# The streams' tile first, the prompt's output projection in the gather rounds: a one-layer encoder step

## The chip, the cores and the metric

The kernel runs on one core of a Trainium2 chip. The metric is device time in microseconds (us). Three executions of the kernel before took 1362.1 us in the median (1358.86 to 1366.68).

## The reference, cut to what matters

384 tokens pass one layer: 256 of a prompt (tiles 0 and 1, of 128 tokens) and 16 each of 8 running streams (tile 2). All is float32.

```
xn = rmsnorm(x);  q,k,v,o,gates, aq,ak,av, iq,ik,iw = split(xn @ w_in)
h_m = mlstm(q, k, v, gates, state) * sigmoid(o)      # 4 heads; new C, n, m are outputs
idx = top_k(indexer scores of iq, ik, iw)            # 64 keys (prompt), 36 (streams)
h_a = softmax(aq . ak[idx] + bias) . av[idx]         # 8 heads, streams with their caches
h   = x + concat(h_m, h_a) @ w_out                   # output projection
hn  = rmsnorm(h)
s   = (hn @ w_pq) . subkeys                          # 8 heads x 2 halves x 128 subkeys
top 16 of each half -> 256 pairs -> top 16 per head  # 128 experts per token, gates by softmax
y   = rmsnorm(h + sum_k gate_k * gelu(pu[e_k] . hn) * pv[e_k])
```

`pu` and `pv` are stored side by side as `peer_uv`, 8 KB per expert. One gather fetches, for each of a tile's 128 tokens, the row of one expert: 1 MB. There are 3 tiles x 128 = 384 gathers, 402.68 MB.

## The kernel before, in words

Everything lives in one arena of on-chip memory with offsets written by hand. The order of the work on each engine is written out; the list `psum_plan` names each use of the six rotating accumulator banks in TensorE's order and which engine reads it (a bank is refilled when the one six names back was read). The last two banks sum up a tile's experts.

*Front.* TensorE turns x, then projects `small` (indexer keys, gates), mq, mk, mv, mo; from then on `head_steps` interleaves the four mLSTM heads (G, ST, NUM, CN) with the projections aq, ak, av, iq. A 128x384 projection group is 8 multiplications (L854), a 128x512 one for mv, mo, av likewise (L860). The indexer, the logits and the softmax of streams and prompt follow, with the output projection's first half `ya` (heads of mLSTM, four multiplications of the eight, L974) of all three tiles between them, then the second half `y`. VectorE computes in that stretch the selections (`keep_top`), the softmaxes, the additions into xr (`add_mix`) and the norms (`norm_h`). `output_gates` (L1320) turns mo of all three tiles in one reciprocal.

*Queries and routing.* `stream_queries` (L1094, `qs`, four chunks of w_pq for tile 2), `scores` (L1103, `sc`) and `prompt_query` (L1112, `qq`, 16 groups for tiles 0 and 1). VectorE's `route_subkeys`, `route_pairs` and `route_experts` turn scores into expert numbers; `route_experts(part)` signals `idx_ok`, at which GpSimd (L621) begins to gather. A part of `PARTS` is (tile, first head, heads): always four heads. ACT takes the exponential of the gates in `gate_exp`, in its order.

*Gather rounds.* Tile 2 goes first (`ORDER = (2, 0, 1)`). Its 16 rounds use 8 slots of 1 MB. For each slot: the gather lands, VectorE's `dots` (L1562), ScalarE's gelu, weight and diagonal (L774, L776, L782), TensorE's `weigh` (L1123: two 128x512 multiplications), then `used` lets GpSimd (L586, L587) gather into that slot again. Ahead of round i TensorE does `query_steps()[i]`, behind the dots of round i VectorE does `routing_steps()[i]`. Tiles 0 and 1 then run in 8 rounds of 16 slots each (GpSimd L604, L610, L611). `finish` adds the sum, norms the tile and releases its output.

A float32 multiplication is two instructions in the profile, so "x8" below is four of them, and a slot's two are "x4".

Of the kernel before, what the change touches and what calls it, by code (L numbers as in the profile page):

```python
# [12 lines left out]
U32 = mybir.dt.uint32  # L13
# [4 lines left out]
P = 128  # L18
# [30 lines left out]
LATE = 5  # L49
# [4 lines left out]

def head_steps():

    return [("G", 0), ("aq", 0), ("G", 1), ("ST", 0), ("aq", 1), ("NUM", 0), ("aq", 2), ("CN", 0), ("aq", 3),
# [3 lines left out]

def psum_plan():
    plan = []

    def add(eng, *names):
        plan.extend((n, eng) for n in names)

    for t in range(NT):
        add("V", f"xT{t}0", f"xT{t}1")
    add("V", "bvec")
    add("A", "small", "mq0")
    add("V", "iw")
    add("A", *[f"mq{g}" for g in range(1, 4)], *[f"mk{g}" for g in range(4)])
    add("V", *[f"mv{t}" for t in range(NT)])
    add("A", *[f"mo{t}" for t in range(NT)])
    add("V", "cols")
    add("A", "winter")  # L80
    add("V", "decay", "mkt0", "mkt1", "mkt2")
    for what, k in head_steps():
        add("A" if what == "ak" else "V", *([f"CN{k}{i}" for i in range(3)] if what == "CN" else [f"{what}{k}"]))
    add("A", "hmT0", "hmT1", "hmT2")

    add("V", "wht", "ri0", "ri1", "ri2", "isc")
    add("A", *[f"rp0{j}" for j in range(JP)])
    add("A", *[f"rp1{j}" for j in range(JP)])

    first, *others = ORDER  # L90
    ya = [f"ya{t}{i}" for t in ORDER for i in range(2)]
    add("V", *ya[:3], "lg0", "lg1", "lg2", *[f"lp0{j}" for j in range(JP)])
    add("V", *ya[3:5])
    add("A", "pTp0", "pTp1", "pTn0", "pTn1", "pp00", "pp01")

    add("V", *[f"lp1{j}" for j in range(JP)], ya[5], "oS0", "oS1", "op00", "op01", f"y{first}0", f"y{first}1")
    add("A", "pp10", "pp11", "pp12", "pp13")
    add("V", "op10", "op11")

    add("A", f"hnT{first}0", f"hnT{first}1", "qs0")  # L100
    add("V", f"y{others[0]}0", f"sc{first}0")
    add("A", "qs1")
    add("V", f"y{others[0]}1", f"sc{first}1", f"y{others[1]}0", f"y{others[1]}1")
    add("A", "qs2")
    for t in others:
        add("A", f"hnT{t}0", f"hnT{t}1")
    for what, *k in sum(query_steps(), []):
        add("V" if what == "sc" else "A", what + "".join(map(str, k)))
# [12 lines left out]

def routing_steps():

    steps = [None, ("subkeys", ORDER[0], 2), ("subkeys", ORDER[0], 3), ("pairs", ORDER[0], 4), ("experts", 1, 4, 4)]
    for n, t in enumerate(ORDER[1:]):
        steps += [("subkeys", t, 0), ("subkeys", t, 1), ("pairs", t, 0), ("experts", 2 + 2 * n, 0, 4),
                  ("subkeys", t, 2), ("subkeys", t, 3), ("pairs", t, 4), ("experts", 3 + 2 * n, 4, 4)]
    assert len(steps) == ROUNDS + LATE
    return steps  # L130

PARTS = [(t, h0, 4) for t in ORDER for h0 in (0, 4)]

# [11 lines left out]
def encoder_kernel(nc, d):  # L147
# [6 lines left out]
    with ExitStack() as ctx:  # L154
# [18 lines left out]
        def over(ap, dim, n):  # L173
# [7 lines left out]
        XR, XN, MIX, RING, CONST = 0, 3072, 6144, 9216, 21504  # L181
        xr = at(XR, NT, DM)
        xnT = at(XN, KC, T)
        mixT = at(MIX, KC, T)
        row = [at(MIX + 384 * i, T, parts=HM) for i in range(8)]
        R_R, R_LF, R_TMP, R_MT, R_MP, R_G, R_WIN, R_WK = row
        AB = 29384

        wslot_at = [RING, RING + 4096, RING + 8192, 44800, 48896]
        wslot = [at(a, KC, 512) for a in wslot_at]  # L190
        w_small = at(RING, KC, WS)
        kiT2 = at(RING, NB, LK)

        wout = [[at(XN + 512 * k, 512) for k in range(4)],
                [at(XN + 2048 + 512 * k, 512) for k in range(2)] + [at(51928 + 512 * k, 512) for k in range(2)]]
        for i in range(2):
            wout[i] += [at(RING + 2048 * i + 512 * k, 512) for k in range(4)]
        KT = at(RING + 1152, JP, NB, LK)
        V = at(RING + 5760, NB, 512)
        workS = at(RING + 9856, LK)  # L200
        negS = at(RING + 10000, LK)
        Lp0 = at(RING + 10144, HA, P)
        relbuf = at(RING + 11168, 2, 512)
        con = {n: CONST + o for n, o in CC.items()}
        ident = at(con["ident"], P)
        tri = at(con["tri"], 512)
        fold = at(RING + 5760, NB, P)
        spread = at(con["spread"], NB, P)
        adm = at(con["adm"], 2, PROMPT)
        blk = at(con["blk"], NB)  # L210
        tmask = at(con["tm"], LS)
        iota = at(con["iota"], PK)
        FOLD = con["fold"]
        HB = FOLD
        hbuf = at(HB, NT, HM, DH)
        o = CONST + NCONST
        mk_tok = at(o, NT, HM, DH)
        gffn = at(o, DM)
        gfin = at(o + 1024, DM)
        ghn = at(o + 2048, 512)  # L220
        gmix = at(o + 2560, KC)
        o += 2568
# [6 lines left out]
        o += 196  # L229
        hs_lo = o  # L230
        headsel = at(o, HM, P, parts=HM)
        smul = at(o + 512, T, parts=HM)
        sadd = at(o + 896, T, parts=HM)
        bgate = at(o + 1280, 2, parts=HM)
        mtl = at(o + 1282, 9, parts=HM)
        o += 1292
        onehot = at(RING + 8192, 511, parts=32)
        relb = at(RING + 8192 + 512, HA, parts=32)
        bvec = at(o, 511, parts=HA)
        o += 512  # L240

        smx = at(o, 3, 3, HA)
        o += 72
        assert o <= AB, o
        aqT = at(AB, JP, PROMPT)
        akT = at(AB + 1024, JP, T)
        iqT = at(AB + 2560, JP, PROMPT)
        ikT2 = at(AB + 3584, T)
        av = at(AB + 3968, NT, 512)
        qbd = at(AB + 5504, JP, NB, 2, LS)  # L250
        qibd = at(AB + 6528, JP, NB, 2, LS)
        MB = AB + 7552
        mqT = at(MB, HM, T)
        mkT = at(MB + 1536, HM, T)
        mv1 = at(MB + 3072, NT, HM, DX)
        mo = at(MB + 4620, NT, 512)
        ogate = at(MB + 4620, NT, HM, DH)
        winb = at(MB + 6156, HM, P)
        arg = at(MB + 6668, 2, 512)
        pT = at(MB + 7692, 2, 512)  # L260
        qd = at(MB + 8716, NB, LK)
        qdf = at(MB + 8716, NB * LK)
        vw = at(MB + 9868, NB + 2, DX)
        CT = at(MB + 11158, HM, NB, DX)
# [1466 lines left out]
```

## Time and profile before

| what | us |
|---|---|
| median of three executions | 1362.1 |
| the profiled execution | 1360.17 |
| its span | 1358.3 |
| first gather issued | 355.58 |
| last expert row landed, about | 1339.0 |

In the profile each engine's busy time is a share of the span. "PEclk" is TensorE's granted clock, as a share of its upper level of 2.4 GHz. The chain of waits is followed back from the last instruction.

### The profile page before, as it was taken

Reading aid. Unit: us, or ns where it says so; the run is one execution under the profiler, and the core shown is the slowest. Engines: PE = TensorE matmul, PEld = TensorE weight load, DVE = VectorE, ACT = ScalarE, POOL = GpSimd, SP = SyncE. Lnnn points to the kernel's source line nnn. Section 1 sums busy time; section 2 is a strip of 40 time slices with the busy share of each in tenths; the row PEclk is TensorE's granted clock in tenths of the full one; section 3 lists DMA queues with packets and bytes.
Section 4 is the critical chain, followed back from the end, with each engine's and each line's share of the span. In section 5 each row is a group of like instructions: output and inputs, shape, how many; then the busy total and the mean of one; then the engine's idle time right before and its main releaser. Section 6 shows DMA issues by size and latency. Waiting matters only on the chain.

```text
span 1358.3 us, 12768 instructions
## 1 busy us (share of the span) xinstructions
PE 1142.0 (84%) x3320; PEld 550.6 (41%) x3320; DVE 798.4 (59%) x1837; ACT 441.0 (32%) x1337; POOL 687.5 (51%) x898
## 2 busy tenths in 40 slices
PE   6999899999999998688776878778777878778776
PEld 4546556477755553233332333222222222222222
DVE  4005534876656777978779786545545545545544
ACT  2101200420232433434335334333334343343343
POOL 0001112000255556665669867777776767767650
PEclk9999899999999999798898889999998999999999
DMA  8321528532489999999999999999999999999995
GB/s 315 112 95 63 103 28 294 224 144 105 183 340 386 366 381 423 378 421 384 412 421 422 421 421 422 422 422 422 422 422 421 422 421 421 422 422 422 422 422 228
DMA packets 68830, 454.91 MB, mean 335 GB/s; under 512 B 7240, under 2 KB 14764, under 8 KB 17328
## 3 DMA queue, kind: packets, MB, share of 16 engines
q0 software_dynamic: 55296, 402.68, 72.0%
q1 hardware_dynamic: 12656, 48.60, 10.5%
q10 hardware_dynamic: 832, 3.08, 0.7%
q8 instruction: 21, 0.34, 0.1%
q14 instruction: 25, 0.20, 0.0%
HBM read 446.62 MB, written 7.71 MB: 334 GB/s over the span
## 4 chain that ended last, share of the span: by engine, by line
DMA 37%; PE 36%; POOL 10%; DVE 7%; issue 5%; ACT 3%; POOLq 0%; SPq 0%; DVEq 0%; ACTq 0%
DMA arena<-in_peer_uv,arena 36%; PE ps L1123 10%; PE ps L854 7%; POOL arena L611 6%; PE ps L860 5%; PE ps L1112 4%; PE ps L974 3%; DVE arena L1562 2%; PE ps L1094 2%; POOL arena L610 2%; ACT arena L782 1%; POOL arena L587 1%; POOL arena L604 1%; DMA arena<-in_w_out 1%; DVE arena L1320 1%
## 5 line engine op out<-in xcount | busy, mean ns | idle before, releaser
L1123 PE MATMUL ps<-arena 128*128 128x512 f32 x1536 | 747.2, 627 | 188.4 <-ACT arena L782 188.4
L1562 DVE CUSTOM_DVE_ANT_0 arena<-arena 128x1024 f32<-128x1024 f32 x384 | 467.0, 1230 | 364.4 <-DMA arena<-in_peer_uv,arena 363.4
L1123 PEld LDWEIGHTS ps<-arena 128*128 128x128 f32 x1536 | 283.3, 196 | 647.1 <-ACT arena L782 362.1
L611 POOL DMA_INDIRECT arena<-in_peer_uv,arena x256 | 304.1, 1188 | 53.2 <-issue 46.7
L774 ACT ACTIVATE arena<-arena 128x1 f32<-128x1 f32 x384 | 77.3, 201 | 477.9 <-DVE arena L1562 477.8
L782 ACT ACTIVATE arena<-arena 128x128 f32<-128x128 f32 x384 | 154.2, 401 | 20.7
L587 POOL DMA_INDIRECT arena<-in_peer_uv,arena x128 | 143.0, 1117 | 27.0 <-issue 21.6
L776 ACT ACTIVATE arena<-arena 128x1 f32 (+1 forms) x384 | 113.0, 294 | 31.4
L854 PE MATMUL ps<-arena 128*128 128x384 f32 (+1 forms) x336 | 112.2, 492 | 0.0
L604 POOL COPY arena<-arena 128x4 uint32 (+1 forms) x64 | 55.6, 869 | 100.8 <-ACT arena L782 100.7
L658 ACT ACTIVATE arena<-ps 128x512 f32<-128x512 f32 (+2 forms) x63 | 30.6, 511 | 231.2 <-PE ps L1112 68.2
L610 POOL TENSOR_TENSOR arena<-arena 128x1 f32<-128x1 f32 x256 | 94.6, 370 | 14.6 <-POOL arena L604 9.1
L854 PEld LDWEIGHTS ps<-arena 128*128 128x128 f32 (+1 forms) x336 | 63.5, 192 | 44.0 <-issue 2.2
L621 POOL MEMSET arena<- 128x1 f32 x1 | 0.1, 98 | 135.3 <-DVE arena L1547 135.3
L860 PE MATMUL ps<-arena 128*128 128x512 f32 x144 | 62.5, 592 | 0.0
L586 POOL TENSOR_TENSOR arena<-arena 128x1 f32<-128x1 f32 x128 | 50.2, 392 | 17.1 <-PE ps L1112 7.7
L575 POOL COPY arena<-arena 128x4 uint32 (+1 forms) x32 | 11.6, 362 | 90.0 <-ACT arena L782 89.9
L538 POOL TENSOR_TENSOR arena<-arena 128x129 f32<-128x129 f32 x8 | 3.0, 400 | 106.8 <-DVE arena L1248 88.8
L1112 PE MATMUL ps<-arena 128*128 128x256 f32 x256 | 56.2, 379 | 0.9 <-ACT arena L658 0.9
L1112 PEld LDWEIGHTS ps<-arena 128*128 128x128 f32 x256 | 48.6, 190 | 9.4 <-issue 1.9
L974 PE MATMUL ps<-arena 128*128 128x512 f32 x96 | 42.5, 593 | 1.0 <-DMA arena<-in_w_out 1.0
L860 PEld LDWEIGHTS ps<-arena 128*128 128x128 f32 x144 | 27.1, 190 | 32.8 <-issue 32.5
(233 smaller groups left out, 759.9 us busy)
## 6 DMA issues: line engine op xcount, KB each, us to landing
arena<-in_w_in SPq DMA_DIRECT2D x8, 2048.0 KB, 7.7
arena<-in_w_pq SPq DMA_DIRECT2D x4, 2048.0 KB, 9.9
arena<-in_peer_uv,arena POOLq DMA_INDIRECT x384, 27.6
arena<-in_w_out SPq DMA_DIRECT2D x3, 1024.0 KB, 7.3
arena<-in_state_C ACTq DMA_DIRECT2D x1, 2064.0 KB, 10.4
out_new_C_s<-arena SPq DMA_DIRECT2D x1, 2064.0 KB, 6.8
arena<-in_cache_k SPq DMA_DIRECT2D x4, 512.0 KB, 7.1
arena<-in_cache_v SPq DMA_DIRECT2D x1, 2048.0 KB, 15.6
```

What stands on the lines that cost most here:

```text
L587: nc.gpsimd.indirect_dma_start(slots[HALF * g + s], None, d["peer_uv"], bass.IndirectOffsetOnAxis(ap=isl[g][:, s:s + 1], axis=0)).then_inc ...
L610: nc.gpsimd.tensor_tensor(pad[:, k:k + 1], pad[:, 0:1], pad[:, 0:1], ALU.mult)
L611: nc.gpsimd.indirect_dma_start(slots[HALF * g + s], None, d["peer_uv"], bass.IndirectOffsetOnAxis(ap=isl[g][:, s:s + 1], axis=0)).then_inc ...
L774: act.activation(gslot[:, s:s + 1], aslot[:, s:s + 1], ACT.Gelu_apprx_tanh).then_inc(ge_ok, 1)
L776: act.activation(wslot_e[:, s:s + 1], gflat[:, t, bass.ds(e0 + s, 1)], ACT.Copy, scale=gslot[:, s:s + 1]).then_inc(w_ok, 1)
L782: act.activation(diag[:, s, :], ident, ACT.Copy, scale=wslot_e[:, s:s + 1]).then_inc(diag_ok, 1)
L854: last = mm(b[0:m, 0:T], w[:, k, lo:lo + m], xnT[:, k, :], start=k == 0, stop=k == KC - 1)
L860: last = mm(b, xnT[:, k, P * t:P * t + P], w[:, k, :], start=k == 0, stop=k == KC - 1)
L974: last = mm(b, mixT[:, k, P * t:P * t + P], wout[i][k], start=k == ks[0], stop=k == ks[-1])
L1112: last = mm(b[:, 0:PROMPT], w[:, k, P * g:P * g + P], xnT[:, k, 0:PROMPT], start=k == 0, stop=k == KC - 1)
L1123: last = mm(ps[:, BANKS + half, :], diag[:, s, :], slots[SLOTS * h + s][:, DM + 512 * half:DM + 512 * half + 512], start=first and s == 0, ...
L1562: v.tensor_tensor_reduce(slots[k][:, 0:DM], slots[k][:, 0:DM], hn[:, t, :], 1.0, 0.0, ALU.mult, ALU.add, aslot[:, s:s + 1]).then_inc(a_ok, 1)
```

## The change

The same mathematics in another order.

- **Front.** Right after `small` come iq, the gate rows, ak, the indexer, aq, the logits, av and the attention of streams and prompt; mv goes between the attention's steps; then mq, mk and mo with the four mLSTM heads. `output_gates` is split: tile 2 alone, later tiles 0 and 1. Only tile 2 has its `ya` and `y` here; its norm, turned rows and stream queries follow.
- **Parts.** Tile 2's first four heads become two parts of two heads. Each is routed in full (subkeys, pairs, experts) before the next; ScalarE reads `qs1` behind `gate_exp(0)` and `qs2` behind `gate_exp(1)`.
- **Rounds of tile 2.** They hold what was ahead: qs3 and the scores of the half 2,3; the output projection of tiles 0 and 1 (now 8 multiplications in one group), their norm, their turned rows, and all 16 `qq`, in the order 8 to 15, 4 to 7, 0 to 3. The prompt's tiles are routed with heads 4 to 7 first. One routing step more goes into tile 0's rounds (`LATE` 6).
- **Loads.** Two of the four chunks of w_pq (2 MB each) are loaded again on SP's queue, in the rounds: `again1` behind y11, `again0` behind qq11. The final gains and, ahead of the rounds, w_pq's last chunk behind the new state's output are also on SP. The bias table comes as two loads into the logits' own place.
- **First slots.** Slots 0 and 1 wait for qs0, 2 and 3 for qs1, 4 to 7 for hmT1 (before: y11, qq3, qq7).

```diff
-LATE = 5
+LATE = 6
-PARTS = [(t, h0, 4) for t in ORDER for h0 in (0, 4)]
+PARTS = [(2, 0, 2, 0), (2, 2, 2, 2), (2, 4, 4, 4), (0, 4, 4, 0), (0, 0, 4, 4), (1, 4, 4, 0), (1, 0, 4, 4)]
 def query_steps():
-    steps = [[("qq", i) for i in range(8)], [("qs", 3), ("sc", ORDER[0], 2), ("sc", ORDER[0], 3)],
-             [("qq", 8), ("qq", 9)], [("qq", 10), ("qq", 11)], [("qq", 12), ("qq", 13), ("sc", a, 0)],
-             [("qq", 14), ("qq", 15), ("sc", a, 1)], [], [("sc", a, 2), ("sc", a, 3)], [], [], [], [],
-             [("sc", b, 0), ("sc", b, 1)], [], [], [("sc", b, 2), ("sc", b, 3)]]
+    steps = [[("qs", 3), ("sc", 2, 3)], [("y", a, 0), ("y", a, 1)], [("y", b, 0), ("y", b, 1)],
+             [("hnT", t, i) for t in (a, b) for i in range(2)] + [("qq", 8)],
+             [("qq", 9), ("qq", 10)], [("qq", 11), ("qq", 12), ("sc", a, 2)], [("qq", 13), ("qq", 14)],
+             [("qq", 15), ("qq", 4), ("sc", a, 3)], [("qq", 5), ("qq", 6)], [("qq", 7), ("qq", 0), ("sc", a, 1)],
+             [("qq", 1), ("qq", 2)], [("qq", 3), ("sc", a, 0)], [("sc", b, 2), ("sc", b, 3)], [("sc", b, 1)],
+             [("sc", b, 0)]]
 def routing_steps():
+    steps = [[("subkeys", 2, 2)], [("subkeys", 2, 3), ("y", a)], [("y", b), ("norm",)], [("pairs", 2, 4)],
+             [("experts", 2)], [("subkeys", a, 2)], [], [("subkeys", a, 3)], [("pairs", a, 4)], [("experts", 3)],
+             [("subkeys", a, 1)], [("subkeys", a, 0)], [("pairs", a, 0)], [("experts", 4)], [("subkeys", b, 2)],
+             [("subkeys", b, 3)]]
+    late = [[("pairs", b, 4)], [("experts", 5)], [("subkeys", b, 1)], [("subkeys", b, 0)], [("pairs", b, 0)],
+            [("experts", 6)]]
...
@@ TensorE, the end of the front
             pe.wait_ge(hn_ok, 1)
-            turn_hn(ORDER[0])
-            was_read(pe, f"hnT{ORDER[0]}1")
+            for i in range(2):
+                turn_hn(2, i)
+            new_state(3)
+            was_read(pe, "hnT21")
             stream_queries(0)
-            was_read(pe, "op11")
-            project_out("y", *tt[2])
-            pe.wait_ge(subk_in, 32)
-            was_read(pe, "qs0")
-            scores(ORDER[0], 0)
+            turn_heads(0)
+            turn_heads(1)
+            pe.wait_ge(subk_in, 16)
+            scores(2, 0)
             stream_queries(1)
-            project_out("y", *tt[3])
-            was_read(pe, "qs1")
-            scores(ORDER[0], 1)
-            for k in tt[4:]:
-                project_out("y", *k)
+            scores(2, 1)
             stream_queries(2)
-            pe.wait_ge(hn_ok, NT)
-            for t in ORDER[1:]:
-                turn_hn(t)
+            scores(2, 2)
...
@@ VectorE, ahead of the rounds
-            add_mix("y", *tt[2])
-            route_subkeys(ORDER[0], 0)
-            route_pairs(ORDER[0], 0, 2)
-            add_mix("y", *tt[3])
-            route_subkeys(ORDER[0], 1)
-            for k in tt[4:]:
-                add_mix("y", *k)
-            norm_h(1, ORDER[1:])
-            route_pairs(ORDER[0], 2, 2)
-            route_experts(0)
+            dve.wait_ge(vals_out, 16)
+            for i in range(2):
+                route_subkeys(2, i)
+                route_pairs(2, 2 * i, 2)
+                route_experts(i)
...
@@ SP, the last loads
+            filled(sp, f"y{ORDER[2]}1")
+            load_w(wbuf["W0"], d["w_pq"][1], "again1")
+            filled(sp, "qq11")
+            load_w(wbuf["PQA"], d["w_pq"][0], "again0")
```

## Rows read from the trace of the kernel before

**Rows 1.** The page: DMA rate in 40 slices; the gathers' queue.
```profile
GB/s 315 112 95 63 103 28 294 224 144 105 183 340 386 366 381 423 378 421 384 412 421 422 421 421 422 422 422 422 422 422 421 422 421 421 422 422 422 422 422 228
...
q0 software_dynamic: 55296, 402.68, 72.0%
```
**Rows 2.** Chain of waits, by engine.
```profile
DMA 37%; PE 36%; POOL 10%; DVE 7%; issue 5%; ACT 3%; POOLq 0%; SPq 0%; DVEq 0%; ACTq 0%
```
**Rows 3.** Stretches: from:to, length, busy (x) per engine, PEclk, DMA share, GB/s.
```profile
139.60:152.00 12.40, 9.43 (x24) 5.76 (x25) 7.66 (x21) 2.58 (x5) 0.00 (x0) 0.72 0.71 205
155.00:226.00 71.00, 71.00 (x252) 42.13 (x251) 28.12 (x64) 5.75 (x11) 17.94 (x18) 1.00 0.44 102
...
230.00:300.00 70.00, 66.17 (x347) 41.44 (x339) 55.62 (x141) 22.48 (x69) 0.00 (x0) 0.98 0.54 213
...
355.60:492.50 136.90, 129.21 (x464) 81.45 (x463) 84.96 (x216) 46.93 (x155) 74.05 (x109) 0.98 0.94 368
492.50:701.00 208.50, 166.70 (x383) 73.00 (x382) 163.38 (x470) 77.80 (x248) 134.58 (x183) 0.91 0.98 401
701.00:1339.00 638.00, 501.03 (x1019) 180.60 (x1018) 367.30 (x704) 248.60 (x782) 450.11 (x572) 0.97 1.01 422
1339.00:1358.30 19.30, 9.81 (x20) 3.28 (x20) 9.05 (x15) 5.08 (x14) 0.00 (x0) 0.87 0.20 82
```
**Rows 4.** Timeline of GpSimd: start, duration, instruction; its first gather.
```profile
355.58 1.16 POOL L587 DMA_INDIRECT arena<-in_peer_uv,arena  x1 [0.45 <-issue]
```
**Rows 5.** The chain of waits in order of time: start, duration, what.
```profile
303.76 7.41 PE ps L1094 x64
311.17 3.44 PE ps L974 x8
...
315.50 7.15 PE ps L1094 x64
```
**Rows 6.** What TensorE waited for, 105 to 355: total, times, longest (first, last).
```profile
PE ps L922 <- DVE arena L1241: 2.9, 1, 2.9
...
PE ps L985 <- ACT arena L658: 0.6, 1, 0.6
```
**Rows 7.** Timeline of TensorE: around its longest wait.
```profile
143.47 1.22 PE L922 MATMUL ps<-arena 128*128 128x256 f32 x2 [2.94 <-DVE arena L1241]
...
145.34 6.89 PE L854 MATMUL ps<-arena 128*128 128x384 f32 x16
...
154.74 5.33 PE L854 MATMUL ps<-arena 128*128 128x384 f32 x16
```
**Rows 8.** Timeline of VectorE: output gates, a norm's start, routing.
```profile
125.82 9.75 DVE L1320 RECIPROCAL arena<-arena 128x1536 f32<-128x1536 f32 x1
...
296.60 1.23 DVE L1430 CUSTOM_DVE_ANT_0 arena<-arena 128x1024 f32<-128x1024 f32 x1
...
315.54 0.70 DVE L1491 MAX8 arena<-ps 128x8 f32<-128x128 f32 x3 [0.20 <-PE ps L1103]
...
320.81 0.76 DVE L1518 TENSOR_TENSOR arena<-arena 128x256 f32<-128x256 f32 x2
...
325.35 0.42 DVE L1501 FIND_INDEX8 arena<-arena 128x8 uint32<-128x256 f32 x1
...
345.05 0.23 DVE L1530 CAST arena<-arena 128x128 f32<-128x128 uint32 x1
...
354.20 0.20 DVE L1547 CAST arena<-arena 128x64 uint32<-128x64 f32 x1
```
**Rows 9.** Timeline of TensorE: rounds of tile 2 with side work.
```profile
442.88 14.00 PE L1123 MATMUL ps<-arena 128*128 128x512 f32 x32 [1.32 <-ACT arena L782]
...
465.12 14.00 PE L1123 MATMUL ps<-arena 128*128 128x512 f32 x32 [0.43 <-ACT arena L782]
...
488.77 20.85 PE L1123 MATMUL ps<-arena 128*128 128x512 f32 x44 [1.86 <-ACT arena L782]
```
**Rows 10.** Timeline of ScalarE at the first round.
```profile
371.96 1.28 ACT L774 ACT_TABLE_LOAD   x1
```

More of the change, by code:

```diff
@@ L69, in add, with heads @@
         plan.extend((n, eng) for n in names)
+    def heads(what, n, *ks):
+        return [f"{what}{k}{i}" for k in ks for i in range(n)]
     for t in range(NT):
@@ L97, in psum_plan @@
-    add("A", "pp10", "pp11", "pp12", "pp13")
-    add("V", "op10", "op11")
-    add("A", f"hnT{first}0", f"hnT{first}1", "qs0")
-    add("V", f"y{others[0]}0", f"sc{first}0")
+    add("A", "small")
+    add("V", "iq0", "iw", "iq1", "iq2", "cols")
+    add("A", "winter")
+    add("V", "decay", "wht", "iq3")
+    add("A", "ak0")
+    add("V", "ri0", "ri1", "ri2")
+    add("A", "ak1")
+    add("V", "isc")
+    add("A", "ak2", "ak3", *heads("rp", JP, 0))
+    add("V", "aq0")
+    add("A", *heads("rp", JP, 1))
@@ new lines, in psum_plan @@
+    add("V", "aq1", "aq2", "aq3", "lg0", "lg1", "lg2", *heads("lp", JP, 0), "av2", "av0")
+    add("A", "pTp0", "pTp1", "pTn0", "pTn1")
+    add("V", "av1", *heads("lp", JP, 1))
+    add("A", "pp00", "pp01")
+    add("V", "mv0", "oS0", "oS1", "op00", "op01", "mv1")
+    add("A", "pp10", "pp11", "pp12", "pp13")
+    add("V", "mv2", "op10", "op11")
+    add("A", "mq0", "mk0")
+    add("V", "G0")
+    add("A", "mq1")
+    add("V", "ST0", "mkt0")
+    add("A", "mk1")
+    add("V", "G1", "NUM0")
+    add("A", "mq2")
@@ new lines, in psum_plan @@
+    add("V", "ST1", "mkt1")
+    add("A", "mk2")
+    add("V", "G2", "NUM1")
+    add("A", "mq3")
+    add("V", "ST2", "mkt2")
+    add("A", "mk3")
+    add("V", "G3", "NUM2", *heads("CN", 3, 0))
+    add("A", "mo2")
+    add("V", "ST3", "mkt3", *heads("CN", 3, 1), "ya20", "ya21", "NUM3")
+    add("A", "mo0", "hmT2")
+    add("V", *heads("CN", 3, 2), "y20", "y21")
+    add("A", "mo1", "hnT20", "hnT21")
+    add("V", *heads("CN", 3, 3))
+    add("A", "qs0", "hmT0", "hmT1")
+    add("V", "sc20")
@@ L102, in psum_plan @@
     add("A", "qs1")
-    add("V", f"y{others[0]}1", f"sc{first}1", f"y{others[1]}0", f"y{others[1]}1")
+    add("V", "sc21")
     add("A", "qs2")
-    for t in others:
-        add("A", f"hnT{t}0", f"hnT{t}1")
+    add("V", "sc22")
     for what, *k in sum(query_steps(), []):
-        add("V" if what == "sc" else "A", what + "".join(map(str, k)))
+        add("V" if what in ("sc", "y") else "A", what + "".join(map(str, k)))
     return plan
@@ L615, in _ @@
             for n, t in enumerate(ORDER):
-                for part, (u, head, heads) in enumerate(PARTS):
+                for part, (u, head, heads, pos) in enumerate(PARTS):
                     if u != t:
@@ L788, in _, with step_exps @@
             steps = routing_steps()
+            def step_exps(i):
+                for what, *k in steps[i]:
+                    if what == "experts":
+                        gate_exp(k[0])
+                    elif what == "norm":
+                        act.wait_ge(ss1, 3 + HM)
+                        act.activation(st[:, 5:7], st[:, 1:3], ACT.Sqrt).then_inc(sq1, 1)
             for n, t in enumerate(ORDER):
@@ new lines, in _, with turn_hn @@
+            head_sum(3)
+            project("mo", 0)
+            turn_heads(2)
+            new_state(2)
+            pe.wait_ge(w_in["low"], 32)
+            was_read(pe, "hmT2")
+            for i in range(2):
+                project_out("y", 2, i)
+            project("mo", 1)
+            def turn_hn(t, i):
+                b = begin(f"hnT{t}{i}")
+                for c in range(4):
+                    k = 4 * i + c
+                    last = nc.tensor.transpose(b[:, P * c:P * c + P], hn[t][:, P * k:P * k + P], ident)
+                end(last)
@@ new lines, in output_gates, with gated @@
+            def output_gates(t0, n):
+                was_read(dve, "mo2" if t0 == 2 else "mo1")
+                dve.wait_ge(ghn_in, 16)
+                m = mo[:, t0:t0 + n, :]
+                link(v.tensor_scalar(m, m, 1.0, None, ALU.add))
+                link(v.reciprocal(m, m))
+                link(v.tensor_tensor(m, m, over(ghn, 1, n), ALU.mult))
+            def gated(t0, n):
+                v.tensor_tensor(hflat[:, t0:t0 + n, :], hflat[:, t0:t0 + n, :], mo[:, t0:t0 + n, :],
+                                ALU.mult).then_inc(hnorm_ok, 1)
@@ L1598, in _ @@
                 dots(0, ORDER[0], i)
-                if steps[i]:
-                    take_step(*steps[i])
+                for step in steps[i]:
+                    take_step(*step)
+            dve.wait_ge(gfin_in, 16)
             finish(0, ORDER[0])
@@ L1608, in _ @@
                         if 2 * i + h < LATE:
-                            take_step(*steps[ROUNDS + 2 * i + h])
+                            for step in steps[ROUNDS + 2 * i + h]:
+                                take_step(*step)
                 with dve.Fori(late, WROUNDS) as i:
```

1129 lines of the change are left out of this document (581 added, 548 removed), and 3 rows, old and new, of the table ORDER.

## The prediction

> **What bounds the kernel now.** I read the rate of the DMA by slice first. From slice 16 on it stands at about 422 GB/s [rows 1], and the stretch 701 to 1339 shows a DMA share of 1.01 [rows 3]: the gathers alone are the bound there. 402.68 MB in 384 gathers at 422 GB/s is 2.485 us each, 954 us in all, 70% of the span of 1358.3. The chain of waits agrees for the end (DMA 37%) and shows that the other great part is TensorE, 36% [rows 2]. So the span is: the time to the first gather, 355.6 us [rows 4], plus 954, plus what the DMA idles in between, plus 19.3 after the last landing [rows 3]. That leaves 1339.0 - 355.6 - 954.2 = 29 us of idling. The rows place it: 368 GB/s in 355.6 to 492.5, 401 in 492.5 to 701, the ceiling after that [rows 3]. In the first of these stretches TensorE is busy 129 of 137 us: with two query groups ahead of a round it needs 22.24 us (442.88 to 465.12) [rows 9] where the DMA needs 8 x 2.485 = 19.9.
>
> Ahead of the first gather TensorE is the bound: 71.0 of 71.0 us busy in 155 to 226 [rows 3], nine waits between 105 and 355 of 9.5 us together (2.9 the longest, 0.6 the shortest) [rows 6].
>
> All is summed against the profiled execution (span 1358.3, 1360.17 in all); the median is 1362.1, so the difference is taken from that.
>
> **1. What leaves the path ahead of the streams' first scores.** Before, `sc20` is done at 315.5 [rows 5]. Nine output groups stand ahead of it (six ya; y20, y21, y00), after the change four. Five groups of 3.44 [rows 5] go: 17.2. The old waits need not come back: 8.6 of the 9.5 us lie ahead of 315.5, the largest behind a reciprocal of 9.75 us over all three tiles [rows 6 to 8], which is split, with mo2 and the heads' products between. After that wait the granted clock was 0.72, between the two levels of 1.2 and 2.4 GHz, and a projection took 6.89 in place of 5.33 [rows 3, 7]; with its small neighbours 2.3 us that also go. Perfectly covered, `sc20` would end at 315.5 - 17.2 - 8.6 - 2.3 = 287.4.
>
> New waits: walking down TensorE's new list with the durations above I find two. The logits now need the reading of aq3 at once (about 1 us), and hmT0 needs VectorE's gates of tiles 0 and 1: two thirds of the reciprocal, 6.5 us, with two passes and the product about 10 us, begun after mo1 is read; `CN3` and qs0 (7.41) [rows 5] cover it but for 1.8. Beyond these I can bound only: nothing, or as much as 15 us, were a quarter of the selections and softmaxes (VectorE is busy 55.6 of 70 us in 230 to 300, and ya covered part) laid bare [rows 3]. The projections ak, aq and av now cover them, by my walk with 5 us or more to spare, so I take 3, nearer to the nothing. The loads are early: at 102 to 205 GB/s [rows 3] the front has DMA to spare. `sc20` ends at 287.4 + 2.8 + 3 = 293.
>
> **2. From the scores to the first gather.** Before: subkeys from 315.54 to 320.8, pairs of two heads to 325.8, experts of four heads from 345.05 to the list at 354.4 [rows 8]; in between lie the second subkeys, the prompt's additions and norm and the other pairs, 39 us in all. Now subkeys 5.3, pairs 5.0, and experts of two heads: 9.35 before, of which 7.8 are six passes over all four heads; half of those and the small rest, 5.5. First gather at 293 + 15.8 + 1.2 [rows 4, 8] = 310, 45.6 us earlier. Its slots are free (qs1 ends at 293 + 7.2).
>
> **3. The first round comes late behind it.** ScalarE's order now puts the gates' exponentials ahead of its readings of qs1 and qs2, so TensorE's sc21 waits for the streams' first pairs, and sc22 for their second. Behind sc20: 5.3 + 5.0 + 1.2, exponential and reading 0.9, sc21 0.9 (what is left of 315.5 - 311.17 behind 3.44 [rows 5]): 13.3. VectorE is through with part 0 at 16.5, with the second subkeys, pairs and first steps of experts at 27.9; sc22 to 29.7; qs3 7.15 [rows 5] to 36.9; reading, table load 1.28 [rows 10] and the first diagonal 2.8 to 39.7. TensorE stands still here for 5.2 and 6.7 us, longer than the 2.94 that brought 2.3 us of slower work [rows 7]: I add 2.3. `weigh` of round 0 begins at 293 + 42 = 335; before it was 374.3, behind eight qq [rows 10]. The eight gathers have by then landed, so the DMA idles.
>
> **4. The rounds.** One round's weigh is 13.8 (half of 27.7; the rows show 14.0 with a modelled end) [rows 9]. Side work of TensorE ahead of rounds 1 to 10: two output groups of 6.87 (twice 3.44), 13.7, in rounds 1 and 2 each; turned rows 1.8, their reading 0.6, one qq 3.46 and a table load's gap 2.6 in round 3; two qq in rounds 4 to 10, which the trace shows as a period of 22.2, with `sc` or without [rows 9]. hn of the prompt is no wait: VectorE has y11 1.4 us after TensorE begins weigh 2, norm (two tiles, two passes of 1.23 each) and ScalarE's root need 7, and weigh 2 lasts 13.8 [rows 8]; the cover is then 5 us. Periods from weigh 0 to weigh 10: 27.5 + 27.5 + 22.4 + 7 x 22.2 + 2.6 (two table loads behind `experts`) = 235.4, so weigh 10 begins at 570.4. VectorE's load in a round is at most 8 x 1.3 for dots and 11 for pairs, 21.5, under the 22.2. The reloads are 4.2 MB, 10 us of DMA; over these ten rounds the DMA has 235 - 10 x 19.9 = 36 us idle, so they cost nothing; were there no such cover, 10 us.
>
> **5. The rest is DMA.** Slot 0 is free 1.7 us after 570.4 and its gather flows 2 us later: from 574 on the DMA has work without a break. Rounds 11 to 15 are 40 gathers, with tiles 0 and 1 296: 296 x 2.485 = 735.6, 1309.6. The same sum for before: refilling after weigh 5, 488.8 + 3.7 = 492.5 [rows 9], 336 gathers 835, 1327.5, and measured 1339.0: 11.5 us were lost, in rounds with pairs and experts on VectorE (three and two of them). One and one are left there: between 0 and 10, I take 5. Last landing 1314.6, plus 19.3: span 1333.9, 24.4 less than before. 1362.1 - 24.4 = 1337.7, rounded 1338.
>
> Of 45.6 us won at the start some 21 are thus given back, because the rounds now are TensorE's for eleven rounds and not for six.
>
> **The clock, by row and by page.** A wait of 2.94 us was followed by slower projections [rows 7]. The Trainium skill (TensorE: Matmul & The Clock Gate, What's actually happening) says that an array left idle falls to half its clock and must be busy again before it is granted the full one; where such a fall comes with each pause, it is paid each time. By the row each of my two long pauses costs 2.3, and I charged one because qs2 lies between them and is waited for anyway. By the rule alone the gaps of 1.3 to 1.9 us ahead of each round might count too, and eleven rounds at 2.3 would cost 25 us more; the rows show rounds behind such a gap at an unchanged 14.0 [rows 9], so the sum stays.
>
 The total is the ceiling of 422 GB/s either way [rows 3].
>
> **The rivals.**
> - *A cleaner front* (0.2): the allowance of 3, part of the named waits and of the 5 do not come: 10 us less, 1328. For it speaks that 155 to 226 shows no wait at all [rows 3]; against it that a hand-made order of this length had nine waits.
> - *Bare attention* (0.22): the front's unseen waits are 15 rather than 3: 1350. The cover of selections and softmax by ak, aq, av is my walk, not a row.
> - *Reloads in full* (0.08): the rounds run by the DMA and not by TensorE, since a slot's way round (landing, dot, weigh, issue) is the limit while SP's queue takes its share; then 4.2 MB cost 10 us: 1348. Against it: the period of 22.2 exceeds 19.9.
> - *Slower: VectorE's chain decides the front* (0.06). The place is the stretch from the indexer scores to the streams' probabilities. If VectorE's 55 us stand there with less than half under projections, TensorE waits 28 us more and the first gather comes at 335; the 21 us given back in the rounds remain, and the time is 1338 + 28 = 1366. It decides from 24 us of unseen waits on.
>
> **How the numbers follow.** Forecast 0.44, rivals 0.2, 0.22, 0.08, 0.06. The forecast's own spread is 8 us either way. Range 1323 to 1355: below it half of the cleaner front's outliers, above it the slower case and the upper end of bare attention. The measurement tells half a per cent, 6.8 us, from no change. Faster (under 1355.3): the first four cases less their tails, 0.88; within: 0.07; slower (over 1368.9): 0.05.
>
> **What would show it.** The first gather near 310; TensorE with two pauses of 5 to 8 us between sc20 and weigh 0; weigh 0 near 335; periods of 27.5 in rounds 1 and 2 and 22.2 in 4 to 10; the DMA under 385 GB/s until 570 and at 422 after. I am wrong on step 1 if the first gather is before 300 or after 320, on step 4 if periods differ by over 1 us, on step 5 if the last landing is more than 742 us behind weigh 10.

## The result: 12.6 us faster, where 24.4 were forecast

| | median, us | lowest to highest | runs | ratio to before (95%) | profiled: span, in all |
|---|---|---|---|---|---|
| before | 1366.68 | 1358.73 to 1368.85 | 11 | | 1358.3, 1360.17 |
| after | 1354.05 | 1351.23 to 1356.22 | 11 | 0.992 (0.9901 to 0.9939) | 1352.2, 1354.05 |

The change is faster, by 0.8%, clear of the noise (the interval ends at 0.9939). The forecast was 1338, a gain of 24.4: the sign was right, and half of the size is missing. The execution of before that I summed against lies at the low end of its spread, so the miss is best read in the span of after, which I had put at 1333.9: 18.3 us.

The page of the kernel after, beside [rows 1, 2]: DMA rate in 40 slices (33.8 us each) and the chain of waits by engine.

```profile
GB/s 177 147 340 169 86 141 0 156 55 288 329 346 332 388 398 382 374 359 397 385 426 425 424 425 425 426 427 426 426 425 425 426 426 427 425 426 426 425 427 245
...
PE 42%; DMA 34%; POOL 8%; DVE 7%; issue 4%; ACT 3%; ACTq 0%; POOLq 0%; SPq 0%; DVEq 0%
```

TensorE's share of the chain grew from 36 to 42% and DMA's fell from 37 to 34%, the direction that step 4 gives. Before, slices 16 and 18 have the full rate, but 17 and 19 have 378 and 384, so the prediction's "from slice 16 on" holds only from 21 on; after, slices 14 to 20 stay at 359 to 398, and from 21 on both are at it. What TensorE waited for ahead of the rounds, beside [rows 6] (total, times, longest):

```profile
PE ps L892 <- DMA arena<-in_w_in: 18.1, 1, 18.1
PE ps L881 <- DVE arena L1273: 11.0, 1, 11.0
PE ps L1179 <- ACT arena L676: 10.7, 2, 5.8
```

The second row is the norm of x at the very start. The third is the two pauses of step 3. The first has no place in my sum: TensorE stands still for 18.1 us because the weights of ak have not landed. The chain in time at that place, and the stretch by the columns of [rows 3]:

```profile
16.95 0.86 SPq L448
17.86 47.69 DMA arena<-in_w_in
...
65.58 6.90 PE ps L892 x16
...
74.58 5.36 PE ps L892 x16
```
```profile
17.00:25.00 8.00, 8.00 (x26) 4.50 (x25) 0.00 (x0) 3.03 (x7) 0.82 (x3) 1.00 0.38 43
...
47.50:65.58 18.08, 0.00 (x0) 0.00 (x0) 0.90 (x3) 0.00 (x0) 0.00 (x0) 0.61 0.59 138
...
699.00:1333.00 634.00, 509.32 (x1032) 186.88 (x1031) 375.88 (x739) 255.15 (x791) 462.83 (x574) 0.96 1.01 426
```

A load of 2 MB takes 47.7 us from issue to landing. The timeline of SP (start, duration of the issue, what) says what stood before it in SP's queue:

```profile
7.61 0.43 SPq L438 DMA_DIRECT2D arena<-in_w_in  x1
16.95 0.86 SPq L448 DMA_DIRECT2D scratch<-arena  x1
17.86 13.18 SPq L438 DMA_DIRECT2D arena<-in_w_in  x1
31.09 4.50 SPq L450 DMA_DIRECT2D arena<-in_cache_kidx  x1
```

L448 stores the bias table to `scratch`, 1024 rows of 2 KB out of 8 partitions. Before it was at 139.4, when all eight loads of w_in had been issued. The change puts it at 16.95, ahead of ak, and merely issuing ak then takes 13.2 us, where the load at 7.61 took 0.43. The first gather, beside [rows 4], and TensorE from `sc20` (309.68) to round 10, beside [rows 5, 9]:

```profile
327.93 1.15 POOL L601 DMA_INDIRECT arena<-in_peer_uv,arena  x1 [0.44 <-issue]
```
```profile
309.68 1.06 PE L1179 MATMUL ps<-arena 128*128 128x128 f32 x8
310.57 7.31 PE L1169 MATMUL ps<-arena 128*128 128x128 f32 x64
...
322.82 2.05 PE L1179 MATMUL ps<-arena 128*128 128x128 f32 x8 [4.94 <-ACT arena L676]
324.66 8.91 PE L1169 MATMUL ps<-arena 128*128 128x128 f32 x64
...
339.33 2.05 PE L1179 MATMUL ps<-arena 128*128 128x128 f32 x8 [5.77 <-ACT arena L676]
341.17 9.17 PE L1169 MATMUL ps<-arena 128*128 128x128 f32 x64
...
353.31 14.00 PE L1200 MATMUL ps<-arena 128*128 128x512 f32 x32 [1.05 <-ACT arena L814]
...
380.88 13.90 PE L1200 MATMUL ps<-arena 128*128 128x512 f32 x32
...
408.35 13.90 PE L1200 MATMUL ps<-arena 128*128 128x512 f32 x32
...
431.30 14.00 PE L1200 MATMUL ps<-arena 128*128 128x512 f32 x32 [2.75 <-ACT arena L814]
453.54 14.00 PE L1200 MATMUL ps<-arena 128*128 128x512 f32 x32 [1.33 <-ACT arena L814]
...
477.19 15.70 PE L1200 MATMUL ps<-arena 128*128 128x512 f32 x32 [1.86 <-ACT arena L814]
...
591.48 17.05 PE L1200 MATMUL ps<-arena 128*128 128x512 f32 x32 [2.75 <-ACT arena L814]
```

From this on the kernel does nearly what the sum said, only later: 42.7 us from `sc20` to `weigh` 0 (42 forecast), periods of 27.6 and 27.5 (27.5), 238.2 from weigh 0 to weigh 10 (235.4), 760.7 from there to the end (763.5).

### The profile page after: what moved, and what is told of

Read it like the earlier page. It is cut to its first block, busy times and chain, and to the rows that moved or that the text cites. A ratio compares the mean times of both kernels' runs of the same rounds, so it can differ in the third digit from the quotient of the medians.

```text
span 1352.2 us, 12839 instructions
## 1 busy us (share of the span) xinstructions
PE 1145.0 (85%) x3320; PEld 557.9 (41%) x3320; DVE 799.5 (59%) x1850; ACT 448.3 (33%) x1346; POOL 691.0 (51%) x898
## 4 chain that ended last, share of the span: by engine, by line
PE 42%; DMA 34%; POOL 8%; DVE 7%; issue 4%; ACT 3%; ACTq 0%; POOLq 0%; SPq 0%; DVEq 0%
DMA arena<-in_peer_uv,arena 30%; PE ps L1200 18%; PE ps L892 6%; PE ps L898 5%; PE ps L1189 4%; DMA arena<-in_w_in 4%; POOL arena L625 3%; PE ps L1112 3%; POOL arena L624 2%; DVE arena L1655 2%; ACT arena L814 1%; POOL arena L618 1%; POOL arena L601 1%; PE ps L1169 1%; PE ps L1044 1%
## 5 line engine op out<-in xcount | busy, mean ns | idle before, releaser
L1200 PEld LDWEIGHTS ps<-arena 128*128 128x128 f32 x1536 | 285.1, 196 | 606.5 <-ACT arena L814 318.4
L601 POOL DMA_INDIRECT arena<-in_peer_uv,arena x128 | 142.6, 1114 | 26.9 <-issue 22.4
L892 PE MATMUL ps<-arena 128*128 128x384 f32 (+1 forms) x336 | 114.6, 498 | 18.3 <-DMA arena<-in_w_in 18.1
L624 POOL TENSOR_TENSOR arena<-arena 128x1 f32<-128x1 f32 x256 | 104.1, 407 | 14.1 <-POOL arena L618 8.3
L600 POOL TENSOR_TENSOR arena<-arena 128x1 f32<-128x1 f32 x128 | 45.9, 359 | 31.9 <-PE ps L1200 26.2
L898 PEld LDWEIGHTS ps<-arena 128*128 128x128 f32 x144 | 27.6, 194 | 31.9 <-issue 31.7
L1169 PE MATMUL ps<-arena 128*128 128x128 f32 x256 | 32.7, 294 | 0.0
```

The source lines that it names most:

```text
L601: nc.gpsimd.indirect_dma_start(slots[HALF * g + s], None, d["peer_uv"], bass.IndirectOffsetOnAxis(ap=isl[g][:, s:s + 1], axis=0)).then_inc ...
L624: nc.gpsimd.tensor_tensor(pad[:, k:k + 1], pad[:, 0:1], pad[:, 0:1], ALU.mult)
L892: last = mm(b[0:m, 0:T], w[:, k, lo:lo + m], xnT[:, k, :], start=k == 0, stop=k == KC - 1)
L898: last = mm(b, xnT[:, k, P * t:P * t + P], w[:, k, :], start=k == 0, stop=k == KC - 1)
L1200: last = mm(ps[:, BANKS + half, :], diag[:, s, :], slots[SLOTS * h + s][:, DM + 512 * half:DM + 512 * half + 512], start=first and s == 0, ...
```

## The experiments

Each result below gives the median, the lowest and the highest time, and the ratio to before with its 95% interval. "By the ratios" means the difference of two ratios times the median of before, which allows for a before that moved a little between the experiments.

Theory Q was: the whole miss is the place of the store in SP's queue. Its rivals: **C**, the new order of TensorE and VectorE has its price at the front anyway, and another wait takes the place of ak's; **D**, the miss lies in the rounds (reloads, prompt's norm). Further questions are what the pauses, the rounds' side work and the split into parts cost. "Before" ran beside each: 1366.1 beside the store behind aq, the store on ScalarE's queue, the store early and the queries first; 1367.6 beside the late reading, the reloads, the thin projection and the part of four; 1366.9 beside the two halves and both kernels with all three.

### The store behind the load of aq

```diff
@@ SP
             was_read(sp, "bvec")
-            sp.dma_start(d["scratch"][:, :, 0:511], over(bvec, 1, P)).then_inc(bvec_out, 16)
             load_w(wbuf["W1"], w_in_of["ak"], "ak")
...
             load_w(wbuf["W2"], w_in_of["aq"], "aq")
+            was_read(sp, "bvec")
+            sp.dma_start(d["scratch"][:, :, 0:511], over(bvec, 1, P)).then_inc(bvec_out, 16)
```

> The changed kernel with one move on SP: the 2 MB store of the bias table to scratch goes behind the load of aq, so ak's load stands ahead of it. Theory Q (queue order): ak waited behind the store (13.2 us to issue, 47.7 us to land); TensorE's wait of 18.1 us for it goes, the first gather comes at about 310 in place of 327.9 and the span falls by 16 to 20 us, to about 1334. Theory V (volume): the 9 MB asked for in 17 to 78 us are too much in any order; then another load is late by as much, the first gather stays within 5 us of 328 and the span within 5 us of 1352.

Measured: 1330.27 (1327.67 to 1333.52), 0.9738 (0.9705 to 0.977), so 23.8 us under the change, by one instruction in another place (20.5 by the spans of the profiled executions, 1352.2 and 1331.7). TensorE's waits up to 345, and its `sc20`:

```profile
PE ps L1180 <- ACT arena L677: 11.7, 3, 5.9
PE ps L882 <- DVE arena L1274: 11.1, 1, 11.1
```
```profile
290.15 1.06 PE L1180 MATMUL ps<-arena 128*128 128x128 f32 x8
```

ak's wait is gone and nothing has taken its place. `sc20` is done at 291.0, where step 1 had 293; the first gather is at 308.4 (310 forecast), weigh 0 at 333.6 (335). The store, at 20.04 in SP's queue, still takes long, and now beside work that doesn't wait for it:

```profile
20.04 2.38 SPq L453 DMA_DIRECT2D scratch<-arena  x1
22.46 50.07 SPq L455 DMA_DIRECT2D arena<-in_cache_k  x4
```
```profile
35.00:45.00 10.00, 10.00 (x46) 6.56 (x45) 2.41 (x10) 2.06 (x4) 1.06 (x1) 0.84 0.47 54
...
55.00:65.00 10.00, 10.00 (x45) 6.81 (x42) 3.63 (x15) 0.49 (x1) 0.00 (x0) 1.00 0.47 53
```

Four loads behind it need 50 us to be issued; while it drains, the DMA moves 54 GB/s at a share of 0.47. I estimate from it some 39 us for the store's 2.09 MB. TensorE is busy all the time.

### The store on ScalarE's queue

```diff
@@ SP
-            sp.dma_start(d["scratch"][:, :, 0:511], over(bvec, 1, P)).then_inc(bvec_out, 16)
@@ ScalarE, behind its reading of bvec
+            was_read(act, "bvec")
+            act.dma_start(d["scratch"][:, :, 0:511], over(bvec, 1, P)).then_inc(bvec_out, 16)
```

> The changed kernel with the same store issued by ScalarE at the same time, not by SP. Theory Q in its narrow form (only the order within SP's queue matters): ak's load issues in under 1 us and lands by 40, the wait of 18.1 us goes, span about 1334 as in the run with the store moved. If instead the store's small packets load the 16 DMA engines themselves, ak lands late though it is alone on its queue: a wait of 5 to 18 us stays, span 1340 to 1352.

Measured: 1329.39 (1328.84 to 1333.72), 0.9748 (0.9716 to 0.978), first gather 302.5. ScalarE issues the store at 18.27, just as SP ends its issue of ak, and ak is in time. That does not yet show ScalarE's queue to be a way out: ak and the store are issued here at the same time; what a store well ahead on the other queue would do, the run doesn't tell. And SP's loads behind the store are held up here too:

```profile
21.10 46.15 SPq L453 DMA_DIRECT2D arena<-in_cache_k  x4
```

46.15 us for the four loads, against 50.07 with the store in SP's own queue and 12.21 in the kernel after, where they are issued from 62.75 on. TensorE doesn't wait for them here either. Whether the price comes from the order in one queue or from the DMA engines that both queues use, no run separates.

### The store early in the kernel before

```diff
             load_w(1)
-            filled(sp, "bvec")
+            was_read(sp, "bvec")
+            sp.dma_start(d["scratch"][:, :, 0:511], over(bvec, 1, P)).then_inc(bvec_out, 16)
             load_w(2)
...
-            sp.dma_start(d["scratch"][:, :, 0:511], over(bvec, 1, P)).then_inc(bvec_out, 16)
```

> The kernel before, with the store of the bias table put where the changed kernel has it (as soon as bvec is read, ahead of the load of mk). Theory Q: mk's load lands near 60 to 65 us and TensorE waits 20 to 28 us for it, so the whole kernel is 18 to 30 us slower than before (about 1385), with no other edit: the cause is the store's place, not the new order. Theory V: the front of this kernel asks for less, so mk is late by under 5 us and the time is within 8 us of before.

Measured: 1389.65 (1385.31 to 1393.19), 1.0169 (1.0128 to 1.0209), 23.5 us slower than before. TensorE's timeline, and SP's:

```profile
65.76 14.58 PE L854 MATMUL ps<-arena 128*128 128x384 f32 x36 [23.71 <-DMA arena<-in_w_in]
```
```profile
16.11 0.86 SPq L451 DMA_DIRECT2D scratch<-arena  x1
17.02 93.31 SPq L443 DMA_DIRECT2D arena<-in_w_in  x5
```

The old order pays for the same place too, 23.7 us of waiting for mk. With the first run this shows from both sides that the store's place makes the wait, and C falls: no other wait took its place.

### The store in two halves

```diff
-            sp.dma_start(d["scratch"][:, :, 0:511], over(bvec, 1, P)).then_inc(bvec_out, 16)
+            sp.dma_start(d["scratch"][:, 0:64, 0:511], over(bvec, 1, 64)).then_inc(bvec_out, 16)
             load_w(wbuf["W1"], w_in_of["ak"], "ak")
...
             load_w(wbuf["W2"], w_in_of["aq"], "aq")
+            sp.dma_start(d["scratch"][:, 64:128, 0:511], over(bvec, 1, 64)).then_inc(bvec_out, 16)
```

Both places that wait for the store wait for both halves.

> The changed kernel with the store in two halves: 64 of the 128 copies in its place, the other 64 behind the load of aq. Theory Q with a price by size: the store drains at some 50 GB/s, 2.09 MB in about 40 us, so half of it leaves ak's load 18 to 22 us sooner: TensorE's wait of 18.1 us falls to 0 to 3, span 1334 to 1338. If the wait has another cause (the position alone, whatever the size), it stays over 12 us.

Measured: 1330.45 (1328.18 to 1333.87), 0.974 (0.9699 to 0.978). SP:

```profile
17.58 0.34 SPq L448 DMA_DIRECT2D scratch<-arena  x1
17.96 0.38 SPq L438 DMA_DIRECT2D arena<-in_w_in  x1
18.38 3.79 SPq L450 DMA_DIRECT2D arena<-in_cache_kidx  x1
```

ak is issued in 0.38 us and TensorE's wait for it is gone; the time is that of the first run, under the 1334 to 1338 that I had expected. The price is not gone but moved down the queue: issuing ak, in_cache_kidx, in_spreads and aq took 13.18 + 4.50 + 11.25 + 15.79 = 44.7 us behind 1024 rows, and takes 0.38 + 3.79 + 4.68 + 15.71 = 24.6 behind 512. All four together pay about by the rows ahead; the first of them does not.

### ScalarE reads the queries first

```diff
-            gate_exp(0)
             stream_queries(1)
-            gate_exp(1)
+            gate_exp(0)
             stream_queries(2)
+            gate_exp(1)
```

> The changed kernel, ScalarE reads qs1 and qs2 ahead of the two exponentials of the gates. If my step 3 holds, TensorE's two waits of 10.7 us together ahead of round 0 fall to under 2, weigh 0 begins 8 to 12 us earlier than 353.3, and since ten rounds behind it are TensorE's, all of it reaches the end: span 1341 to 1345. Rival: round 0 then waits for VectorE (experts of part 1, then the dots), and the gain is under 4 us.

Measured: 1350.65 (1348.56 to 1353.79), 0.9901 (0.987 to 0.9931), 3.4 us under the change by the medians and 2.6 by the ratios, with intervals that overlap. I had expected 1341 to 1345: a miss, and the rival's size. The pauses shrink, but a new one comes ahead of round 0:

```profile
PE ps L1200 <- ACT arena L814: 5.5, 1, 5.5
PE ps L1179 <- ACT arena L676: 4.9, 3, 3.4
```

Weigh 0 is 8.2 us earlier (345.13) and weigh 10 only 6.1 (585.36); 1.0 us of both is there at `sc20` already. TensorE is ready sooner than the first slots' weights, so a part of what the pauses had cost becomes the wait of 5.5 us. ScalarE waits there in its turn for VectorE, whose dots come behind the routing, and the weighing behind the wait takes 16.06 us in place of 14.00.

### One reading of a round goes behind its first weights

On the first run's kernel. ScalarE reads a round's last `qq` after the weights of slots 0 and 1, in rounds 3 to 10 (the diff shows the place only):

```diff
...
                 for s in range(SLOTS):
+                    if s == 2 and late_read is not None:
+                        read_qq(late_read)
...
```

> On the kernel with the store moved (1330.3): in rounds 3 to 10 ScalarE reads the last qq of a round behind the weights of slots 0 and 1, not ahead of them. Theory T (TensorE bounds the ten rounds, step 4): the gaps of 0.4 to 2.8 us ahead of each weigh, 12.2 us together, go, the period falls from 22.2 to about 20.9, weigh 10 begins 9 to 12 us earlier and the end comes 8 to 11 us earlier: about 1321. Rival D (the DMA, slowed by the reloads, is as near a bound): weigh 10 gains, but the end less than 4 us.

Measured: 1320.54 (1319.42 to 1327.94), 0.9675 (0.9645 to 0.9705), 9.7 us under the first run (8.6 by the ratios). Rounds 5, 6 and 10:

```profile
445.36 7.03 PE L1210 MATMUL ps<-arena 128*128 128x512 f32 x16
...
470.79 13.90 PE L1210 MATMUL ps<-arena 128*128 128x512 f32 x32
...
556.32 14.00 PE L1210 MATMUL ps<-arena 128*128 128x512 f32 x32 [1.02 <-ACT arena L819]
```

Weigh 0 (327.46) to weigh 10 is 228.9 in place of 238.2. The periods of rounds 0 and 1 stay at 27.6 and 27.5; from round 2 on they are 20.0 to 21.8, but for 25.4 from round 5 to 6, where half of the slots are weighed one by one. What step 4 took as TensorE's own period of 22.2 held a gap of 0.4 to 1.9 us, its wait for ScalarE.

### Without the reloads

On the first run's kernel: both reloads are left out, and the eight groups that would use them multiply with another chunk.

> On the kernel with the store moved: the two reloads of w_pq (4.2 MB) are left out and eight query groups use chunk 2 instead (the prompt's experts are then others). Theory T: the reloads stood in idle time of the DMA, so weigh 10 and the end move by under 2 us. Rival: they cost their 10 us of DMA, the end comes 8 to 10 us earlier.

Measured: 1329.55 (1328.02 to 1333.42), 0.973 (0.9709 to 0.9751); weigh 0 to weigh 10 238.2, as with them. The reloads cost nothing that can be measured here. D falls in this half.

### A thin output projection

On the first run's kernel: one multiplication in place of eight in each group of the prompt's output projection.

> On the kernel with the store moved: the prompt's output projection in rounds 1 and 2 is one multiplication per group in place of eight (the prompt's h is then another); additions, norm and everything else stay. Theory T: TensorE's 24 us leave, the two rounds fall from 27.5 to the DMA's 19.9, weigh 10 begins 13 to 16 us earlier and the end comes 12 to 16 us earlier: about 1316. Rival D: the end moves by under 5 us.

Measured: 1326.43 (1323.68 to 1327.96), 0.9697 (0.9679 to 0.9716), 3.8 us less (5.6 by the ratios), weigh 0 to weigh 10 234.1. I had expected 13 to 16: a miss. TensorE from round 2 to 3, and VectorE in it:

```profile
384.87 1.98 PE L1201 MATMUL ps<-arena 128*128 128x512 f32 x4 [0.33 <-ACT arena L815]
390.64 2.75 PE L1161 MATMUL ps<-arena 128*128 128x128 f32 x16 [3.78 <-DVE arena L1552]
...
402.70 2.84 PE L1201 MATMUL ps<-arena 128*128 128x512 f32 x6 [2.75 <-ACT arena L815]
```
```profile
382.59 1.23 DVE L1656 CUSTOM_DVE_ANT_0 arena<-arena 128x1024 f32<-128x1024 f32 x1 [1.25 <-DMA arena<-in_peer_uv,arena]
...
388.10 2.48 DVE L1552 SCALAR_TENSOR_TENSOR arena<-arena 128x1024 f32<-128x1024 f32 x2
```

Once TensorE's share goes, single slots (x4 is one slot) pace rounds 1 and 2, and the prompt's norm becomes a wait of 3.8 us. The norm stands in VectorE's order behind the last dot of round 2, and this dot waits for its gather (382.59); in the change the two projections had covered both, as step 4 said. All of the gain, 4.1 us, is in weigh 0 to weigh 3 (73.9 in place of 78.0). So removing the work of the two long rounds brings about 4 us, not the 21 that I said were "given back". Where the rest of those 21 lies was not measured.

### The first part with four heads again

On the first run's kernel: one routing of four heads; ScalarE reads `qs1` first.

```diff
-PARTS = [(2, 0, 2, 0), (2, 2, 2, 2), (2, 4, 4, 4), (0, 4, 4, 0), (0, 0, 4, 4), (1, 4, 4, 0), (1, 0, 4, 4)]
+PARTS = [(2, 0, 4, 0), (2, 4, 4, 4), (0, 4, 4, 0), (0, 0, 4, 4), (1, 4, 4, 0), (1, 0, 4, 4)]
...
```

> On the kernel with the store moved: tile 2's first four heads are one part again, so the first gather waits for both subkeys and pairs and four heads of experts: it comes 12 to 15 us later (about 322). ScalarE reads qs1 ahead of the gates' exponential. Theory W (what counts is when round 0's weigh begins, not the first gather): weigh 0 still begins near 333 and ends 0 to 4 us later, the end comes 0 to 4 us later. Rival G (each us of the first gather counts, as the sum of gathers suggests): 12 us later, about 1342.

Measured: 1335.34 (1334.38 to 1339.89), 0.9773 (0.975 to 0.9796), 5.1 us over the first run. GpSimd's first gather:

```profile
318.75 1.16 POOL L602 DMA_INDIRECT arena<-in_peer_uv,arena  x1 [0.44 <-issue]
```

Counted from the end of `sc20` (287.5 here, 291.0 in the first run, see the section on the prediction), the first gather is 13.9 us later, weigh 1 4.1 and weigh 10 5.9, of which 1.7 are one weighing that took 15.70 in place of 14.00. In round 0 the slots are now weighed one by one. So splitting the part is worth some 4 to 5 us of the 14 by which it brings the first gather forward, and G, each us of the first gather counts, falls.

### All three, twice

The store behind aq, the readings first and the late reading together; then the same with the store on ScalarE's queue.

> Three edits together: store behind aq, ScalarE's readings of qs1 and qs2 ahead of the exponentials, last qq of a round read late. Against the kernel with store and late reading (1320.5) the reading order should bring 3 to 5 us, as it did alone (1354.1 to 1350.7): about 1316, 2.5% under the changed kernel's 1354 and 3.5% under the kernel before. If the first round now waits for VectorE alone, it brings nothing and the time is 1320.

> As the kernel with all three edits, but the store is issued by ScalarE right behind bvec's reading. Alone it was as good as the store behind aq (1329.4 against 1330.3), so the same time within 3 us: about 1316.

Measured: 1316.96 (1316.05 to 1319.54), 0.9641 (0.9609 to 0.9673), and 1319.16 (1313.1 to 1325.1), 0.9673 (0.964 to 0.9706): the same within what is measured. The first is 37.1 us under the change, the best kernel of this study. On top of the late reading (1320.54) the readings first bring 3.6 us by the medians, but the intervals overlap and the traces don't show it: weigh 10 begins at 555.72 against 556.32, and both spans are 1317.6 to 1317.7. That they bring anything on top is not shown.

## Why the prediction missed by half

**Step 1 failed**, in one sentence: "The loads are early: at 102 to 205 GB/s [rows 3] the front has DMA to spare." `sc20` was done at 310.6 and not 293, and the first gather at 327.9 is past the 320 that the prediction had named as its sign of being wrong on this step. The first run, without the wait, has 291.0: the store's place costs 19.6 us there, 18.1 of waiting and 1.5 for the slower projection behind it (6.90 against 5.36).

That 291.0 is near 293 is luck. In eight other kernels of this study without the wait for ak, `sc20` is done at 285.1 to 287.8. The first run and after both have a stretch in which the granted clock is 0.50, the level of 1.2 GHz, though the profile shows TensorE busy throughout and no wait of it from 120 to 200. In the chain of after the same 16 instructions take 1.70 us ahead of it and 3.25 in it:

```profile
161.75 1.70 PE ps L1044 x16
...
169.08 3.25 PE ps L1044 x16
```

The stretch is 167.9 to 176 in after and costs 5.1 us; in the first run it is 148.7 to 157 and costs 5.2. The kernel with the late reading has the same front and no such stretch (1.00 from 120 to 200), and 285.9. So the rest of step 1 was 7.1 us too high: the named waits (2.8), the allowance (3) and 1.3 more did not come. The 17.6 of step 1 are 19.6 for the store, plus 5.1 for this stretch, less 7.1. With the store moved the gain is 35.8 us (1366.1 to 1330.3); the rival "a cleaner front" had put it at 34.

I used the mean rate of a stretch as if it priced a DMA. It does not: the rate was 43 GB/s just when ak could have flowed, with a share of 0.38. And I had listed the loads as "early" without walking SP's list as I walked TensorE's. The trace of before held the price. SP's timeline there, at the store's old place:

```profile
139.42 0.86 SPq L456 DMA_DIRECT2D scratch<-arena  x1
140.33 15.53 SPq L458 DMA_DIRECT2D out_new_m<-arena  x1
```

A store of 0.1 KB took 15.5 us to be issued, because of what stood ahead of it. Had I read that row, with the store's new place from the diff, a rival "ak comes late" would have had a time.

**Steps 2 and 3 held.** From `sc20` to the first gather 17.3 us (17.0 forecast), to weigh 0 42.7 (42). The pauses were 4.94 and 5.77 (5.2 and 6.7). I charged slower work once, 2.3; it came behind both: 2.05 and 8.91 against 1.06 and 7.31, and 2.05 and 9.17, 2.6 and 2.8 us. The Trainium skill's rule (TensorE: Matmul & The Clock Gate, What's actually happening) was right against my choice here for pauses of 5 us. For the rounds' gaps the row was right only in part: behind 1.33 and one gap of 2.75 they kept their 14.00, but the one behind 1.86 took 15.70, and weigh 10, behind another 2.75, took 17.05, with a granted clock of 0.50 over its first 4.5 us.

**Step 4 held**, 238.2 against 235.4: the first two periods within 0.1 of 27.5, the third 22.95 (22.4), then 22.2 four times and 23.7, 23.9 and 23.7, where I had 2.6 for two table loads. The 23.9 is 1.7 over its 22.2, more than the 1 us that the prediction allowed, and holds the weighing at 477.19; this is 1.7 of the 2.8. The reloads are free, as the run without them shows. The sentence on where the 45.6 us went was wrong in its reason, as the thin projection shows.

**Step 5 held, by two errors against each other.** Behind weigh 10 2.8 us less than forecast. The gathers flowed at 426 and not 422 GB/s, 2.465 us each, 6 us less over 296; the loss in rounds with routing was about 8 and not 5, counted to the same gather as there. The "last landing 1339.0" of before was in fact the fourth from last: its last dot begins at 1346.38, the tail behind the last landing is 12 us, and the DMA idled 36 us and not 29. The same 19.3 stands in both sums and cancels. The sign "more than 742 us behind weigh 10" did not fit the prediction's own sum, which gives 1314.6 - 570.4 = 744.2; measured to the same gather it is 741.5.

The sum: 17.6 + 0.7 + 2.8 - 2.8 = 18.3, the miss in the span. By the medians it is 11.8 (24.4 less 12.6), since before's profiled execution was quicker than its median and after's was at it. Of the rivals none was this: "bare attention" gives nearly its time, 1350, by another cause, which the first run excludes.

## What to carry to other kernels

When a change moves a DMA in a queue, read that queue's own timeline, duration of issue by duration of issue, and write down what is behind it; a mean rate says nothing of a store from few partitions. Such a store goes behind the loads that someone will wait for. That another engine's queue avoids the price is not shown: ak was in time there because it was issued together with the store, and SP's four loads behind them took 46 us to be issued. And a step's cost in a pipeline is not its own duration: taking out some 24 us of multiplications (twice 13.7, less an eighth) brought 4, because slots and a norm stood right behind. Last, compare stages from a common event, as here from the end of `sc20`, and look in more than one trace: a stretch of slow clock that came in some executions only moved everything behind it by 5 us.

## What was not expected of the hardware

- The store of 1024 rows of 2 KB from 8 partitions ran at 53 to 54 GB/s with a DMA share of 0.47. The Trainium skill (DMA: Bandwidth & Descriptors, Why a DMA increments its semaphore by 16 and not by 1) says that a DMA is spread over as many engines, at most 16, as divide the slowest dimension of both its sides; 8 partitions give 8 engines, and the share, near a half, agrees.
- The DMA behind it took 13.2 us to be issued, 0.38 behind a store of half as many rows; with the next three DMAs it was 44.7 and 24.6 us. With the store on the other queue, four loads on SP took 46.15.
- With TensorE idle for 18.1 us the granted clock was 0.61 of 2.4 GHz over the wait and 0.50, the level of 1.2 GHz, from 55 to 65; the projection behind it took 6.90.
- The clock fell to the lower level in the middle of work too: behind rows of 16 multiplications of 128x32, with no wait of TensorE from 120 to 200, it was 0.50 for some 8 us in the first run and in after, shorter in others, and not at all with the late reading and in both kernels with the store on ScalarE's queue. No run here says why.
- The gathers of the last 634 us flowed at 426 GB/s in after and in the best kernel, 422 in before [rows 3]. No run here says why.
